# A hybrid decoder step: first stage rebuilt around wide modulation units, with the first norm applied per partition as turned rows leave PSUM

## The reference, cut to what matters

```python
mod = silu(c) @ w_ada + b_ada            # 9 rows; w_ada: 1024 x 6144
sh1, sc1, ga1, sh2, sc2, ga2 = split(mod, 6)
h = rms_norm(x, g_norm1) * (1 + sc1) + sh1
q, k, v, f, u, gate_b, gate_c = split(h @ w_in)
attn = attend(q, k, v, log_sigmoid(f + b_forget))
x = x + ga1 * merge_heads(attn, short_conv(gate_c * u), gate_b) @ w_out
h = rms_norm(x, g_norm2) * (1 + sc2) + sh2
x = x + ga2 * moe(h)                     # 32 experts, top 2 of 8 in one of 4 groups
y = rms_norm(x, g_final) * (1 + scf) + shf   # a modulation of its own
```

## Time and profile before

| | |
|---|---|
| three runs | 1039.85, 1045.21, 1049.06 us; median 1045.21 |
| span of the profiled execution | 1045.5 us (the page gives no other time for it) |
| busy: PE, VectorE, ScalarE, POOL | 847.3 (81%), 542.3 (52%), 202.7 (19%), 292.1 (28%) us |
| DMA | 318.40 MB, mean 305 GB/s |

### The profile page before, as it was taken

How to read it: one execution, slowest core, us unless ns; L and a number is a source line. 1 busy time by engine, 2 the same in 40 slices (tenths; PEclk the granted TensorE clock), 3 DMA queues, 4 the chain that set the end, 5 groups by cost and what they waited for, 6 DMA issues and landing times.

```text
span 1045.5 us, 10030 instructions
## 1 busy us (share of the span) xinstructions
PE 847.3 (81%) x3810; PEld 371.9 (36%) x3810; DVE 542.3 (52%) x726; ACT 202.7 (19%) x385; POOL 292.1 (28%) x261
## 2 busy tenths in 40 slices
PE   7689999999457899998987989765888888778810
PEld 1144443444222334443232333223444444444300
DVE  1379999999999999642042020542111111111258
ACT  1321112100342322242000000121211222111111
POOL 4417632562101213102233232301222222221013
PEclk9689999999666575566999798876999999999955
DMA  9928778886779996616986999968999999999242
GB/s 332 399 90 290 285 281 340 275 304 207 261 276 335 371 382 249 222 41 256 361 341 267 359 333 358 373 254 294 389 410 413 412 411 412 412 412 413 107 176 82
DMA packets 79514, 318.40 MB, mean 305 GB/s; under 512 B 11090, under 2 KB 11110, under 8 KB 58473
## 3 DMA queue, kind: packets, MB, share of 16 engines
q1 hardware_dynamic: 52592, 163.56, 40.7%
q0 software_dynamic: 24576, 150.03, 38.3%
q10 hardware_dynamic: 2308, 4.31, 1.1%
HBM read 307.17 MB, written 14.85 MB: 308 GB/s over the span
## 4 chain that ended last, share of the span: by engine, by line
PE 65%; DMA 13%; DVE 11%; issue 6%; ACT 4%; SPq 1%; POOL 0%; ACTq 0%; POOLq 0%; DVEq 0%
PE bank L406 15%; PE bank L740 9%; PE bank L609 5%; PE bank L764 5%; DMA R_kv<-in_cache_v_dram,kv_index 5%; DMA R_w<-in_w_expert_up_dram 5%; PE bank L560 5%; PE bank L305 3%; PE bank L480 3%; PE bank L477 3%; PE bank L498 2%; DVE R_x L1232 2%; ACT R_h L861 2%; DMA R_w<-in_w_ada_dram 2%; DVE R_cm L1238 2%
## 5 line engine op out<-in xcount | busy, mean ns | idle before, releaser
L1732 POOL DMA_INDIRECT R_kv<-in_cache_k_dram,kv_index x64 | 98.6, 1540 | 244.6 <-DVE R_cm L1238 221.3
L1232 DVE TENSOR_TENSOR R_x<-R_kv,R_x 128x1024 f32<-128x1024 f32 x128 | 161.5, 1302 | 3.8 <-DMA R_x<-q_rows_scratch 3.8
L1238 DVE TENSOR_REDUCE R_cm<-R_x 128x16 f32<-128x1024 f32 x128 | 149.5, 1208 | 0.0
L406 PE MATMUL bank<-R_h,R_w 128*128 128x512 f32 x320 | 140.2, 599 | 1.2 <-ACT R_h L861 1.2
L1732 POOL DMA_INDIRECT R_kv<-in_cache_v_dram,kv_index x64 | 63.1, 986 | 166.3 <-PE bank L560 146.4
L560 PE MATMUL bank<-R_kv,R_cm 128*8 128x512 f32 x512 | 75.9, 676 | 19.8 <-DMA R_kv<-in_cache_v_dram,kv_index 19.6
L1808 POOL DMA_INDIRECT expert_rows_scratch<-R_h,R_part x32 | 32.0, 1001 | 211.6 <-DVE R_h L1593 204.2
L406 PEld LDWEIGHTS bank<-R_h,R_w 128*128 128x128 f32 x320 | 61.0, 192 | 79.9 <-issue 78.3
L1590 DVE COPY R_h<-bank 128x128 f32<-128x128 f32 x32 | 9.3, 292 | 147.0 <-PE bank L756 147.0
L305 PE MATMUL bank<-R_w,R_q 128*32 128x512 f32 x256 | 51.8, 938 | 13.8 <-DMA R_w<-in_w_ada_dram 8.2
L1593 DVE TENSOR_SCALAR R_h<-bank,R_part 128x512 f32<-128x512 f32 x32 | 24.0, 751 | 70.6 <-PE bank L764 70.6
(11 more groups left out here) (329 smaller groups left out, 1345.0 us busy)
## 6 DMA issues: line engine op xcount, KB each, us to landing
R_w<-in_w_ada_dram SPq DMA_DIRECT2D x24, 1024.0 KB, 8.1
R_w<-in_w_in_dram SPq DMA_DIRECT2D x12, 1024.0 KB, 7.7
R_w<-in_w_ada_final_dram SPq DMA_DIRECT2D x8, 1024.0 KB, 10.2
R_kv<-in_w_expert_gate_dram SPq DMA_DIRECT2D x8, 1024.0 KB
R_kv<-in_w_expert_up_dram SPq DMA_DIRECT2D x8, 1024.0 KB
R_kv<-in_w_expert_down_dram SPq DMA_DIRECT2D x8, 1024.0 KB
R_q<-in_w_expert_gate_dram SPq DMA_DIRECT2D x8, 1024.0 KB
R_q<-in_w_expert_up_dram SPq DMA_DIRECT2D x8, 1024.0 KB
```

What stands on the lines that cost most here:

```text
L406: last = nc.tensor.matmul(bank[m][:, :], l, r, start=(k == 0), stop=(k == KD - 1))
L1232: V.tensor_tensor(prod[:, r, :], kv_ring[:, n % RING, r, :], spread(q, [P, CH // 2, HW]), ALU.mult)\
L1238: V.reduce_sum(scores[:, b, lo:lo + CH // 2, :], prod[:, r, :].rearrange("p r (h d) -> p r h d", h=H), AX.X).then_inc(S["k_used"], 1)
L1732: pool.indirect_dma_start(kv_flat[:, g % RING, :], None, k_rows if g < NKV else v_rows, bass.IndirectOffsetOnAxis(kv_index[:, n:n + 1], 0))\
```

## The change

The first eight units become wide: one block of 128 rows by 2048 columns each (8 KB pieces), all eight accumulated in one bank; so do the 24 later ones (three groups of eight). The nine rows of the first modulation are turned by four PE transposes, so that shift and scale stand on partitions (`mod_t`, `sc_t`). VectorE only multiplies x by rstd; PE turns the rows block by block (`turn_prompt(k)`, all four tiles), and scale and shift are applied as the block leaves PSUM, on ScalarE for even k and VectorE for odd k. The sample queries are spread to 128 partitions by eight matmuls (`query_rows`) and evicted to SBUF. SP issues units 0 to 9 ahead of the prompt's x; ScalarE's queue takes six small loads. POOL's gathers begin when seven units are used, and POOL waits for the turned rows ahead of the fifth. Of twelve later modulation evictions three are left; the last also waits for 48 key chunks.

The core of the diff:

```diff
-        sh1_p, sc1_p, sh1_s, sc1_s, g1_b = (view(R_q, i * 1024, [1024]) for i in range(5))
-        part_a = view(R_q, 5120, [4, 512])
-        x_a = view(R_x, 0, [5, D])
+        mod_a = view(R_q, 5120, [512])
+        mod_t = view(R_q, 5632, [16, B + 1])
+        sc_t = view(R_q, 5792, [KD, B + 1])
+        x_a = view(R_cm, 0, [NT, D])
+        x_s = view(R_x, 4096, [D], B)
...
+        part = [view(R_part, lo, [SECS]) for lo in (5120, 5632, 2560)]
+        part_01 = view(R_part, 5120, [2, SECS])
...
+            def ada_unit(i, psum):
+
+                u, k = (i if i < KD else 12 + i), i % KD
+                pe.wait_ge(unit_loaded[u % 3], 16 * (u // 3 + 1))
+                for j in range(4):
+                    last = nc.tensor.matmul(psum[32 * j:32 * j + 32, :], c_t[:, k, :], w_flat[:, u % 3, j * SECS:(j + 1) * SECS],
+                                            start=(k == 0), stop=(k == KD - 1 and i >= KD))
+                last.then_inc(S["unit_used"], 1)
...
+            def turn_samples():
+
+                pe.wait_ge(S["h_row_ready"], 1)
+                for k in range(KD):
+                    last = nc.tensor.transpose(bank[6][:, 64 + 8 * k:72 + 8 * k],
+                                               h_row[0][0:B, k * P:(k + 1) * P], ident[0:B, 0:B])
                 last.then_inc(S["h_psum"], 1)
+                pe.wait_ge(S["vec_loaded"], 80)
+                nc.tensor.transpose(bank[6][:, 128:156], vec_rows[:, :], ident[0:28, 0:28]).then_inc(S["setup_psum"], 1)
+
+            for k in range(KD):
+                ada_unit(k, bank[0])
+                if k == KD - 3:
+                    turn_samples()
+            for j in range(4):
+                last = nc.tensor.matmul(bank[0][32 * j:32 * j + B + 1, :], ones[0:1, 0:B + 1],
+                                        b_row_a[:, j * SECS:(j + 1) * SECS], start=False, stop=True)
+            last.then_inc(S["ada_done"], 1)
+            pe.wait_ge(S["part_ready"], 1)
+            for c in range(4):
+                last = nc.tensor.transpose(bank[1][:, c * P:(c + 1) * P], mod_a[:, c * P:(c + 1) * P], ident[:])
+            last.then_inc(S["setup_psum"], 1)
+
+            def turn_prompt(k):
+
+                pe.wait_ge(S["h_row_ready"], 5)
+                if k >= 4:
+                    pe.wait_ge(*((S["ht_dve"], (k - 2) // 2) if k % 2 else (S["ht_act"], (k - 2) // 2)))
+                for t in range(NT):
+                    last = nc.tensor.transpose(bank[k % 4][:, t * P:(t + 1) * P], x_a[:, t, k * P:(k + 1) * P], ident[:])
+                last.then_inc(S["h_psum"], 1)
+
+            def query_rows(b):
+
+                if b >= 2:
+                    pe.wait_ge(S["qb_ready"], b - 1)
+                nc.tensor.matmul(bank[4 + b % 2][:, :], sel[:, b, :], s_part[:, 0, :], start=True, stop=True)\
+                    .then_inc(S["q_spread"], 1)

...
-            transpose_h(0)
             sample_section(0)
+            pe.wait_ge(S["samp_evac"], 1)
+            pe.wait_ge(S["consts_ready"], 4)
+            query_rows(0)
+            query_rows(1)
             sample_rows(0)
-            for i in range(1, 5):
-                transpose_h(i)
-            pe.wait_ge(S["ht_ready"], 5)
+            for k in range(KD):
+                turn_prompt(k)
+                if k >= 2:
+                    query_rows(k)
+            pe.wait_ge(S["ht_act"], 4)
+            pe.wait_ge(S["ht_dve"], 4)
+            pe.wait_ge(S["qb_ready"], B)
             prompt_section(0)
...
+            def spread_pair(j):
+
+                q, g = divmod(j, 4)
+                rows = slice(32 * g, 32 * g + 32)
+                nc.tensor.matmul(bank[6][0:B, :], sel[rows, 0:B, 0], part[q][rows, :], start=True, stop=True)
+                nc.tensor.matmul(bank[7][:, :], sel[rows, B, :], part[q][rows, :], start=True, stop=True)\
+                    .then_inc(S["expand_done"], 1)
+
...
+            act.dma_start(x_s[:, :], x_sample.rearrange("b t d -> (b t) d")).then_inc(S["xs_loaded"], 16)
...
+            act.dma_start(vec_rows[20:28, :], g_norm1.rearrange("l (k p) -> (l k) p", p=P)).then_inc(S["vec_loaded"], 16)
+            act.dma_start(b_f[:, :], b_forget.rearrange("l h -> h l")).then_inc(S["vec_loaded"], 16)
...
+            act.wait_ge(S["xs_loaded"], 16)
+            act.wait_ge(S["consts_ready"], 2)
+            step(nc.scalar.activation(junk[0:B, :], x_s[:, :], ACT.Square, accum_out=ssq[0:B, NT:NT + 1]))
+            nc.scalar.activation(ssq[0:B, NT:NT + 1], ssq[0:B, NT:NT + 1], ACT.Sqrt, bias=eps[0:B, 0:1], scale=1.0 / D)\
+                .then_inc(S["rstd_sq"], 1)
+            act.wait_ge(S["x_loaded"], 16)
+            for t in range(NT):
+                step(nc.scalar.activation(junk[:, :], x_a[:, t, :], ACT.Square, accum_out=ssq[:, t:t + 1]))
+            nc.scalar.activation(ssq[:, 0:NT], ssq[:, 0:NT], ACT.Sqrt, bias=eps[:, 0:1], scale=1.0 / D)\
+                .then_inc(S["rstd_sq"], 1)
+
+            act.wait_ge(S["samp_done"], 1)
+            copy(s_part[:, 0, :], bank[7][:, :]).then_inc(S["samp_evac"], 1)
+
+            def query_out(b):
+                act.wait_ge(S["q_spread"], b + 1)
+                copy(q_b[:, b, :], bank[4 + b % 2][:, :]).then_inc(S["qb_ready"], 1)
+
+            def prompt_out(k):
+                jj, cc = divmod(k, 4)
+                act.wait_ge(S["h_psum"], k + 2)
+                nc.scalar.activation(h_t[:, k, 0:T], bank[k % 4][:, :], ACT.Identity, scale=sc_t[:, k, B:B + 1],
+                                     bias=mod_t[:, 4 * cc + jj, B:B + 1]).then_inc(S["ht_act"], 1)
+
...
+            act.wait_ge(S["hs_ready"], 1)
+            for k in range(KD):
+                if k % 2 == 0:
+                    prompt_out(k)
+                if k >= 2:
+                    query_out(k)

...
-            def ada_evac(n):
-                act.wait_ge(S["ada_done"], 4 + n + 1)
-                copy(part[:, n, :], bank[7][:, :]).then_inc(S["part_ready"], 1)
+            def ada_evac(q):
+                act.wait_ge(S["unit_used"], 14 + KD * q)
+                if q == 3:
+                    act.wait_ge(S["k_used"], 2 * 6 * NCH)
+                copy(part[q - 1][:, :], bank[7][:, :]).then_inc(S["part_ready"], 1)

...
-            step(V.reciprocal(rstd[:, :], ssq[:, :]))
-
-            dve.wait_ge(S["g_loaded"], 16)
-            for m in range(2):
-                dve.wait_ge(S["expand_done"], m + 3)
-                lo = slice(m * SECS, (m + 1) * SECS)
-                V.scalar_tensor_tensor(sc1_s[0:B, lo], bank[2 + m][0:B, :], 1.0, g1_b[0:B, lo], ALU.add, ALU.mult)
-                step(V.scalar_tensor_tensor(sc1_p[:, lo], bank[4 + m][:, :], 1.0, g1_b[:, lo], ALU.add, ALU.mult))
-            dve.wait_ge(S["sh_ready"], 2)
-            for i in range(5):
-                t, n = (NT, B) if i == 0 else (i - 1, P)
-                sc, sh = (sc1_s, sh1_s) if i == 0 else (sc1_p, sh1_p)
-                if i >= 2:
-                    dve.wait_ge(S["h_psum"], i - 1)
-                r = h_row[i % 2]
-                step(V.scalar_tensor_tensor(r[0:n, :], x_a[0:n, t, :], rstd[0:n, t:t + 1], sc[0:n, :], ALU.mult, ALU.mult))
-                V.tensor_tensor(r[0:n, :], r[0:n, :], sh[0:n, :], ALU.add).then_inc(S["h_row_ready"], 1)
-
-
+            step(V.reciprocal(rstd[0:B, NT:NT + 1], ssq[0:B, NT:NT + 1]))
+            V.tensor_scalar(h_row[0][0:B, :], x_s[:, :], rstd[0:B, NT:NT + 1], None, ALU.mult).then_inc(S["h_row_ready"], 1)
+            dve.wait_ge(S["setup_psum"], 3)
+            V.tensor_copy(vecs[:, :], bank[6][:, 128:156]).then_inc(S["setup_ready"], 1)
+            dve.wait_ge(S["ada_done"], 1)
+            V.tensor_copy(mod_a[:, :], bank[0][:, :]).then_inc(S["part_ready"], 1)
+            dve.wait_ge(S["setup_psum"], 4)
+            step(V.tensor_copy(mod_t[:, :, :], bank[1][:, :].rearrange("p (i r) -> p i r", r=32)[:, :, 0:B + 1]))
+            mod_c = mod_t[:, :, :].rearrange("p (c j) r -> p c j r", j=4)
+            for jj in range(2):
+                g1 = vecs[:, 20 + 4 * jj:24 + 4 * jj].rearrange("p (c o) -> p c o", o=1)
+                last = V.scalar_tensor_tensor(sc_t[:, 4 * jj:4 * jj + 4, :], mod_c[:, :, 2 + jj, :], 1.0,
+                                              spread(g1, [P, 4, B + 1]), ALU.add, ALU.mult)
+            step(last)
+            xn = bank[6][:, 64:128].rearrange("p (k n) -> p k n", k=KD)
+            step(V.tensor_tensor(h_t[:, :, T:T + B], xn, sc_t[:, :, 0:B], ALU.mult))
+            for jj in range(2):
+                hs = h_t[:, 4 * jj:4 * jj + 4, T:T + B]
+                last = V.tensor_tensor(hs, hs, mod_c[:, :, jj, 0:B], ALU.add)
+            last.then_inc(S["hs_ready"], 1)
+            dve.wait_ge(S["rstd_sq"], 2)
+            step(V.reciprocal(rstd[:, 0:NT], ssq[:, 0:NT]))
+            for t in range(NT):
+                V.tensor_scalar(x_a[:, t, :], x_a[:, t, :], rstd[:, t:t + 1], None, ALU.mult).then_inc(S["h_row_ready"], 1)
+            for k in range(1, KD, 2):
+                jj, cc = divmod(k, 4)
```

(64 more changed lines are left out.)

198 lines of the change are left out of this document (59 added, 139 removed).

## The result

The changed kernel takes 1067.3 us (median of four runs, 1066.1 to 1068.5); the kernel before, on the same chip, 1042.5. The ratio is 1.023 with a 95% interval of 1.019 to 1.027. The forecast was 1047.0, within 1%. The change is 24.8 us slower.

A forecast was written before the change was run, and what follows sets the result against it. The prediction took VectorE to have no slack from the first key product until 335 us. A start 3.7 us later less 2.0 us gained in attention made +1.7 us on the median: 1047.0 us, range 1035 to 1058.

The forecast's parts named there:

- Spreads from 32 rows stream the same 512 columns: 0.: Later modulation, after the first stage: spreads reading 32 rows were priced at no change, 0 us.
- The start: First stage: x lands at 47 and the first key product comes at 68.4 instead of 64.69, 3.7 us later.
- Rival A: First stage: x comes early, at 36 rather than 47, VectorE starts at 57.4, total 1036 us; chance 0.21.
- under the 2.49, so three buffers suffice: First stage: PE uses a wide unit in 1.94 us, under its 2.49 us transfer, so three buffers are enough.
- rival B: Turns and spreads between x and section 0: PE stays at half clock, total 1055 us; chance 0.14.
- The 2.0 us for the attention: Attention, 335 to 445 us: a removed PE stall and fewer ScalarE evictions gain 2.0 us, bounded by 0 and 5.
- the stall of 2.5 us at 387: Attention: PE waits 2.53 us for a unit whose 2 KB packets took turns with 8 KB gathers; counted in the gain.

The follow-up runs named there:

- second execution: The changed kernel run again, unedited: 1067.5 us, ratio 1.024 to the kernel before.
- both repairs: Changed kernel, with gathers waiting for x and later spreads taking all 128 rows against a zero-padded weight table, result unchanged: 1045.0 us, ratio 1.000.
- x ahead of unit 8: Kernel with both repairs, and SP issues x ahead of units 8 and 9 instead of behind them: 1037.6 us, once more 1037.0.
- longer ring: Version with x ahead of unit 8, plus two more buffers, so units 3 and 4 are issued without a wait: 1034.1 us, ratio 0.992.
- the run with narrow pieces: Version with x ahead of unit 8, each of the first eight units loaded by four transfers in 2 KB pieces: 1035.7 us, ratio 0.992.

## Why the prediction was wrong

*The step that failed* is the last sentence of the part on what comes after the first stage: "Spreads from 32 rows stream the same 512 columns: 0." It priced a matmul by its columns alone. The spread itself does cost the same, 1.0 and 1.1 us in both traces; its price is the clock of the matmuls behind it. That is 13.9 us in the changed kernel and 14.4 the other way round in the kernel before, more than half of the 24.8. Without it the changed kernel measured 1053.6, inside the 1035 to 1058. No rival had it, and none could have come from it: they all were about the first stage or about waits. The windows of before did show one of the places: from 335 on PE runs at a clock of 0.62, between its two levels. The prediction used the clock for the new turns, but not for the operations whose shape the change alters. The Trainium skill, "TensorE: Matmul & The Clock Gate", section "Part 1: The HAM clock gate (the "warmup" mystery)", says that the gate goes by how busy PE has been. By that, if busy means that PE has matmuls to run, the two kernels would have the same clock in the last experts, where their matmuls are the same and their pauses nearly (1.16 us before and 0.95 after, ahead of the first expert's matmuls); the runs with 32, 64 and 128 rows show 0.88, 0.93 and 1.00, so here the measurement decides.

*The start* came out by the mechanism that was forecast, and a little later: +4.7 us where +3.7 had been worked out (69.4 against 68.4; 70.6 in the second execution). x shares the DMA engines with the gathers and lands last; ScalarE waits for it and only then evicts the queries; from there three matmuls take 4.7 (5.0 forecast) and the turns and spreads 8.8 to the first product (10.8). That the sum came so near is in part luck: x was 3.4 us later than forecast, and the steps behind it 2.3 quicker. (Two slips of 0.1 change nothing: 57.6 + 9.9 is 67.5, and 1045.2 + 1.7 is 1046.9.) Rival A, x early, had in the trace of before all that its price needs, and the run in which gathers wait for x is that rival made true: 9.0 us. What spoiled it are the gathers that run beside x; whether the old gate, one unit later, would have been enough was not run.

*The sizes* of three terms were off. x lands at 50.4, not 47, because units are 3.0 us apart ((27.99 - 7.26) / 7), not 2.49: "under the 2.49, so three buffers suffice" compared PE's use with the transfer and forgot that a buffer is also empty from the issue to the landing. The trace of before had numbers for it: 7.44 us in the chain for the second unit, which also waits for the first, and a median of 6.0 from issue to landing from 5 to 20 us; even (6.0 + 1.94) / 3 is 2.65, above 2.49. In the changed kernel SP issues units 3 to 7 some 7.0 us before PE uses them, and (7.0 + 1.9) / 3 is the 3.0 that was measured. Bridging at half clock (rival B) did not happen: the first two spreads were at half clock and the turns at full. The 2.0 us for the attention can't be told from the scatter of executions: the stall of 2.5 us at 387 is gone (PE waits for no unit there any more), and from the first key chunk to 520 us the traces of versions with full rows move against that of before by +0.9 (both repairs), +2.7 (x ahead of unit 8), -3.9 (128 rows in the changed kernel) and -4.2 (longer ring). PE's clock in that stretch differs from one to the next.

*What stays open*: the version with both repairs starts its key chunks 3.7 us sooner than the profiled execution of before and has the same median. Part of this is that execution: the run of the kernel before with spreads from 32 rows, whose first stage is unedited, has its first key product at 62.95 and not at 64.69. The rest, some 2 us, is within the interval of that ratio (3 us to either side), and no run was made for it. In the same way the spreads' 14 us and a start that is 5 to 8 us later (69.4 and 70.6, against 64.69 and 62.95) make 19 to 22 of the 24.8; the rest is within the scatter of executions and is not explained further.

## What to carry to other kernels

Where PE is the bound, an edit to the shape of a matmul is priced by the time of the matmuls after it too, not by its own alone; here streaming 128 rows instead of 32 was worth 14 us, and a small table of zeros makes that possible without changing the result. What a stage waits for should be issued alone: transfers that are not needed yet are to be held back by the landing of the one that is. For a ring of buffers, compare (issue to landing + use) / buffers with the transfer time: here 3.0 us for three buffers against 2.49, and with five the units came 2.5 us apart. The number to compare comes from the landings, not from the rate, and it goes with the transfers: narrow pieces came 2.69 us apart in the same three buffers.

## What the runs showed of the hardware that was not expected

From the first of the last six pairs of spreads to the end of PE's work there are the same matmuls in every kernel. With 128 rows this took 48.4 to 49.4 us (the kernel before and every version with full rows), with 64 rows 51.5, with 32 rows 55.4 to 55.6, in two different kernels; behind three of the six pairs from 32 rows the granted clock falls to its lower level in the middle of an expert's matmuls, behind two of the six from 64 rows, and behind none from 128. Rows with weight zero count as rows (1.00 in the version with both repairs). And in a ring of three, units in 2 KB pieces came closer together than in 8 KB pieces (2.69 us and 3.04), though the rates of the earlier trace rows differ by 8% the other way. The Trainium skill, "DMA: Bandwidth & Descriptors", section Specifications, puts line rate at pieces of 512 B and more. Where the engines were full, from 9 to 24 us, this case differs: 2 KB pieces moved 367 GB/s in the run with narrow pieces (their packets fill 101.6% of the window), and 8 KB pieces almost alone 419 with the longer ring (100.4%), so here the measurement decides.
